# VectorE takes the adaptive tiles in steps 10 to 33 of the attention in place of steps 34 to 57

## What is computed

```python
shift, scale, gate = jnp.split(jax.nn.silu(c) @ w_ada + b_ada, 3, axis=-1)
h = rmsnorm(x, g_norm) * (1 + scale) + shift
z = h @ w_in                       # one projection, split among all heads
oa = mla_attend(...)               # branch A: 8 heads, chunk-causal, low-rank q and kv
ob = dsa_attend(...)               # branch B: 8 heads over the top-k keys of an indexer, with a bias
m = sigmoid(ma) * ((oa * silu(ga)) @ w_oa) + sigmoid(mb) * ((ob * silu(gb)) @ w_ob)
x = x + gate * (m @ w_out)
```

## Time and profile before

| what | us |
|---|---|
| median of three runs | 1259.64 |
| profiled execution: span | 1255.0 |
| TensorE busy | 1131.9 (90%) |
| VectorE busy | 783.6 (62%) |
| ScalarE busy | 486.3 (39%) |
| GpSimd busy | 388.6 (31%) |
| adaptive products in both layers (L1480, 96 instructions) | 128.3 |
| row maximum of step 10, 33, 34 in layer 1 | at 294.79, 370.97, 373.83 |
| the same in layer 2 | at 885.54, 961.72, 964.59 |

### The profile page before, as it was taken

One profiled execution on the slowest core, in us unless ns is written; L12 is line 12 of the kernel. 1 busy time (PEld: TensorE's weight loads), 2 busy tenths in 40 slices (PEclk: granted clock), 3 DMA queues, 4 the chain that ended last, 5 costly groups with the idle time before them and its releaser, 6 DMA issues. The chain is left out here.

```text
span 1255.0 us, 20340 instructions
## 1 busy us (share of the span) xinstructions
PE 1131.9 (90%) x7644; PEld 982.9 (78%) x7660; DVE 783.6 (62%) x1626; ACT 486.3 (39%) x1088; POOL 388.6 (31%) x220
## 2 busy tenths in 40 slices
PE   3189999999999999989979999999999999988996
PEld 2067698677888888879967779777888888878995
DVE  7964899572447875254646489965235786535555
ACT  4344545532443333332324544633244343332322
POOL 5633265021122322233334235502112222223332
PEclk9589799999999999989999989999999999999998
DMA  9624022121114444113424303221111454311353
GB/s 376 220 87 132 14 88 68 55 68 34 34 34 152 153 155 155 60 40 115 166 99 128 91 19 100 64 63 47 34 42 53 156 173 152 118 51 51 110 179 150
DMA packets 39066, 128.17 MB, mean 102 GB/s; under 512 B 5736, under 2 KB 6344, under 8 KB 38128
## 3 DMA queue, kind: packets, MB, share of 16 engines
q1 hardware_dynamic: 36496, 122.04, 29.5%
q10 hardware_dynamic: 2464, 4.74, 1.0%
HBM read 117.41 MB, written 11.58 MB: 103 GB/s over the span
## 5 line engine op out<-in xcount | busy, mean ns | idle before, releaser
L688 PE MATMUL pj<-h_hi,w_hi 128*128 128x272 f32 x1776 | 526.4, 296 | 13.3 <-DVE h_lo L1488 6.1
L690 PE MATMUL pj<-h_lo,w_hi 128*128 128x272 f32 x1776 | 517.3, 291 | 0.0
L689 PE MATMUL pj<-h_hi,w_lo 128*128 128x272 f32 x1776 | 514.4, 290 | 0.0
L1591 POOL TENSOR_TENSOR w_lo<-ring,w_hi 128x1024 fp32r<-128x1024 f32 x112 | 275.6, 2461 | 584.7 <-ACT w_hi L1033 584.6
L688 PEld LDWEIGHTS pj<-h_hi,w_hi 128*128 128x128 f32 x1776 | 339.0, 191 | 17.4 <-POOL w_lo L1591 6.6
L689 PEld LDWEIGHTS pj<-h_hi,w_lo 128*128 128x128 f32 x1776 | 339.0, 191 | 0.2
L690 PEld LDWEIGHTS pj<-h_lo,w_hi 128*128 128x128 f32 x1776 | 337.7, 190 | 0.0
L1033 ACT ACTIVATE w_hi<-ring 128x1024 fp32r<-128x1024 f32 x112 | 119.1, 1063 | 144.1 <-PE pj L690 130.8
L1480 DVE CUSTOM_DVE_ANT_0 squares<-ring,silu_c 128x1024 f32<-128x1024 f32 x96 | 128.3, 1336 | 7.0 <-DMA ring<-in_wts 5.3
L1179 ACT ACTIVATE probs<-logit,negmax 128x128 f32<-128x128 f32 (+2 forms) x68 | 39.1, 575 | 198.9 <-DVE negmax L1422 184.9
L1413 DVE TENSOR_REDUCE negmax<-ps 128x1 f32<-128x128 f32 (+1 forms) x64 | 31.4, 490 | 107.1 <-PE ps L883 106.9
(11 more groups left out here) (239 smaller groups left out, 1541.6 us busy)
## 6 DMA issues: line engine op xcount, KB each, us to landing
ring<-in_wts SPq DMA_DIRECT2D x167, 512.0 KB, 3.6
wide<-x_between SPq DMA_DIRECT2D x4, 1088.0 KB, 5.6
x_between<-wide ACTq DMA_DIRECT2D x16, 272.0 KB, 2.5
wide<-in_wts SPq DMA_DIRECT2D x3, 1024.0 KB, 20.8
ring<-in_wts SPq DMA_DIRECT2D x6, 384.0 KB, 2.9
wide<-in_xT SPq DMA_DIRECT2D x1, 2176.0 KB, 13.2
x_between<-in_xT SPq DMA_DIRECT2D x1, 2176.0 KB, 9.8
bias_p<-in_wts SPq DMA_DIRECT2D x2, 1024.0 KB, 7.8
```

What stands on the lines that cost most here:

```text
L688: pe.matmul(out, hi, h_hi[:, k, half(b)], start=(k == first), stop=False)
L689: pe.matmul(out, lo, h_hi[:, k, half(b)], start=False, stop=False)
L690: return pe.matmul(out, hi, h_lo[:, k, half(b)], start=False, stop=(k == stop))
L1591: pool.tensor_tensor(w_lo[:, slot, :], w(*splits[n]), w_hi[:, slot, :].bitcast(F32), ALU.subtract).then_inc(s_wlo, 1)
```

## The change

The constant that says in which step the first adaptive tile is taken goes from 34 to 10.

```diff
@@ -70,7 +70,7 @@
 QI_LAG = 3
 EARLY_GB = 2
 FIRST_DSA = 2 + NH * NQ
-ADA_STEP = 34
+ADA_STEP = 10
 
 RING = 3
 SLOT = 1024
```

## The result

The changed kernel takes **1324.99 us** (median of four runs, 1317.8 to 1328.1) against 1259.77 for the kernel before: 1.0505 times as long, interval 1.0472 to 1.0537. The forecast was 1307 in a range of 1295 to 1320. The direction was right, the rise is 65 us in place of 47.6, and the time lies 5 us above the range.

What follows compares the result with a forecast made beforehand. TensorE was taken to bound branch B, and VectorE, with tiles, steps 14 to 33. Step 33 comes 24.3 us a layer later, 0.5 is given back: 2 x (24.3 - 0.5) = 47.6 us, hence 1307 us, range 1295 to 1320.

Steps and rivals of the forecast that it cites:

- TensorE bounds branch B, tiles are free there: Attention's second branch, where the tiles were: TensorE busy 114.37 of 115.17 us, so adaptive tiles cost nothing there.
- 0.5 us a layer: Steps 34 to 57: time given back by taking the tiles out, between nothing and 0.8 us.
- A tile is 2.49 us, VectorE's own work 14.57 us a head, VectorE becomes the bound: Steps 14 to 33: with four tiles a head VectorE needs 3.64 us a step against TensorE's 2.79.
- GpSimd's low parts, 6.0 us a layer: Steps 13 to 33: five low parts hold off VectorE's scalings, 6.0 us a layer, between 0 and 12.
- The ring, no wait: Tile loads, each waiting for the tile three before: just in time, no wait; bounds 0 and 3.8 us for each of four.
- 1.7 us of pure delay: Steps 10 to 13: the copy of the sample's values (L1444) starts 1.7 us later, and TensorE waits for it.
- TensorE has no way round it: its transposes need the scaling: Steps 14 to 33: TensorE must wait for the scaling of the step before and can't run further ahead.
- Rival B: Steps 10 to 33: TensorE's clock falls to 1.2 GHz, up to 39 us a layer more, 1385 us; chance 0.07.
- A: The forecast itself: VectorE bounds steps 14 to 33 at about 3.6 us a step, plus held scalings; chance 0.82.
- C: Late loads keep VectorE waiting 8 us or more a layer, 1323 us or more; chance 0.06.
- D: Relief of VectorE in steps 34 to 57 gives back more than the first branch costs, 1236 us; chance 0.02.
- E: No effect: the tiles fit in the waits of the first branch, or a smaller rise, to 1280; chance 0.03.

Runs made afterwards that it cites:

- start40: Kernel before the change with the adaptive tiles starting at step 40 (steps 40 to 63) instead of 34; 1261.6 us against 1260.3, ratio 0.9993.
- all_three: Changed kernel plus dummy matmuls on TensorE, head outputs taken before the tile's second product, and five low parts over 64 columns; 1291.5 us.
- shortlow: Changed kernel with the five low parts of tiles split in steps 13 to 33 made over 64 of 1024 columns; 1318.0 us, ratio 1.0462.
- noload: Changed kernel without the adaptive tiles' loads; VectorE's products read the silu(c) vectors instead; 1323.2 us, ratio 1.0501.
- warm: Changed kernel with dummy matmuls on TensorE where it waits for VectorE's outputs; 1303.8 us, ratio 1.0361.
- two: Changed kernel with outputs taken before the tile's second product and five low parts over 64 columns, no dummy matmuls; 1303.2 us.
- outfirst: Changed kernel with VectorE's outputs taken between the two products of the previous step's tile, not behind the whole tile; 1317.3 us, ratio 1.0438.
- half_two: Changed kernel with each tile's second product over 64 of 1024 columns, early outputs and low parts over 64 columns, no dummy matmuls; 1282.6 us.
- proj_first: Kernel before the change with step 12's projection moved ahead of TensorE's wait for the copy of the sample's values (L1444); 1255.8 us, ratio 0.9950.

## Why the prediction was wrong

The sum went wrong by one thing: it priced all of TensorE's work in steps 10 to 33 at the clock that it had before, and held against a fall that the idle pieces would be under 2 us. Both of these steps failed, the first most of all in steps 10 to 13. Part by part:

- **TensorE bounds branch B, tiles are free there**: right, and `start40` shows no difference for other places. **"0.5 us a layer" comes back**: not so, nothing does. The pace is 19.29 us a head with and without tiles; 19.18 was the one head behind the last tile, misread as a pace. Branch B's 0.8 us only makes up for the longer step 33, which the sum had unchanged at 2.86 us.
- **A tile is 2.49 us, VectorE's own work 14.57 us a head, VectorE becomes the bound**: right. VectorE is busy 59.4 to 63.3 us in steps 16 to 33, and `all_three` runs them in 61.1 to 62.2 us against the 62.5 summed.
- **GpSimd's low parts, 6.0 us a layer**: the mechanism right, the size 3.3 to 3.9 by `shortlow`. In the trace of layer 1 the 1.92 of step 19 is 1.46, the 1.79 of step 24 is 1.44 and the 0.98 of step 29 is 0.33; the one of step 14 is missing.
- **The ring, no wait**: right, 0.6 us in all and no change in `noload`.
- **Steps 10 to 13, "1.7 us of pure delay"**: this step failed, and it holds 10.6 of the 18 us that the six stretches of the two layers took beyond the forecast. It followed VectorE's queue and priced what stands behind L1444 at the length it had before. Those matmuls were to run after longer waits, and took 11.4 in place of 8.2 us; in layer 2 the values ahead of them were slow too. Measured: 5.7 us in layer 1 and 8.3 in layer 2. With `warm` it was 1.0 (clock 1.00) and 2.5 (clock 0.92), one on either side of the 1.7.
- **"TensorE has no way round it: its transposes need the scaling"**: incomplete. The values of a new head need the output of the old one (`first_of_use` and `s_oev` in the code), and that output stands behind a tile. Of the 24.2 us that TensorE waited for VectorE in layer 1, 13.2 are for L1464 and 4.2 for L1473. These are the long pauses.
- **Rival B, the tensor clock**, was given 0.07 with "the idle pieces here will be under 2 us". The longest were 4.2, 3.1 and 2.8 us, because of the line above. But the argument fails even where its condition holds: in steps 16 to 33 no wait of `two` is over 1.7 us and none of `outfirst` over 2.1, and the granted clock is 0.89, and 0.85 and 0.83. Nor is B a rival to A, which it was set against: both are true at once, VectorE is the bound and the low clock adds to it. `warm` puts it at 21 us of the 65. TensorE's slack didn't cover it: `two` and `all_three` differ by 3.6 us a layer. The prediction's own figure for it ("a third of the time at half clock is mostly covered by TensorE's slack and gives some 1312 to 1330") holds the measured time, but the range was cut at 1320 because the case was thought unlikely.
- Rivals C, D and E: excluded by `noload`, by branch B's pace, and by the result.

In short: 47.6 forecast, some 43 measured once the clock is held up (1303.8), and some 21 for a clock that falls. What in TensorE's waits brings the clock down, their length, their number or the kind of work between them, no run here separates. The Trainium skill (TensorE: Matmul & The Clock Gate, section "What's actually happening"), which was cited beside rival B, left both outcomes open. The trace has now decided for this stretch: the clock falls, with TensorE busy 51.82 of 68.88 us.

## What to carry to other kernels

Work that is free under a bound engine isn't free one stage earlier: read the pace with and without it from the trace, over several heads, and remember that two nearly equally loaded engines with a short lead over each other take longer than the busier of them needs in all (53.7 and 55.9 us for 48 to 49 in `half_two`), so that even work that would fit in the sum of the waits costs. When an engine is made to wait, look up every semaphore on which the other one depends, the release of its output banks too, and price TensorE's work behind a new pause at both clock levels. Where TensorE must wait, something harmless to multiply can shorten the whole (21 us here); real work moved ahead of the wait did too (4 us, `proj_first`).

## What the runs showed of the hardware that was not expected

- Added matmuls made the kernel faster: 92 dummies a layer (128x384, bf16), 21 us less in all, with the granted clock up from 0.80, 0.88 and 0.93 to 1.00 in the three stretches of layer 1, and from 0.69, 0.77 and 0.93 to 0.92, 1.00 and 0.97 in those of layer 2.
- A new wait of 1.7 us at L935, and one of 1.4 in place of 0.8 us ahead of L955, went with 2.5 us more for L955's 32-column matmuls (6.39 against 3.94 us), at a clock of 0.56 against 0.96.
- The clock fell without a wait of over 1.7 us: to 0.89 in steps 16 to 33 of `two`, with TensorE busy 53.45 of 64.74 us.
- The clock also costs when another engine is the bound: 3.6 us a layer between `two` and `all_three`, and in steps 16 to 33 VectorE waits 3.7 and 2.4 us for scores in `two`, 1.1 and 0 in `all_three`.
- GpSimd and VectorE hold each other off until the instruction that is running ends, as in the earlier trace rows, also when VectorE's is a short scaling: 1.75 in place of 0.29 us. The row maximum ahead of it, which reads PSUM, wasn't held by the same low part (346.22, 0.42 us as elsewhere).
